# A third PSUM bank for the dilated heads' results, and the pair's transposes through one bank, a chunk every second step

## The chip, the cores and the metric

The kernel runs on one core of one Trainium2 chip. The metric is the device time in microseconds (us) of one execution; lower is better.

## The reference

One layer of a decoder trunk on `x` (1, 2048, 1024), fp32. `h = layer_norm(x)`, one projection `h @ w_in` is cut into the queries, keys and values of two mixers and a gate:

```python
proj = einsum('btd,dc->btc', h, w_in)
qa, ka, va, qb, kb, vb, gate = split(proj)
ya = dilated_mixture(heads_a(qa), heads_a(ka), heads_a(va), rel_bias)   # 8 heads of 64
yb = stick_breaking(heads_b(qb), heads_b(kb), heads_b(vb))              # 8 heads of 64
y = concatenate([ya, yb]) * silu(gate)
out = einsum('btc,cd->btd', y, w_out) + b_out
return layer_norm(ALPHA * h + out)
```

`dilated_mixture` runs every head in three configurations (window, dilation) = (128, 1), (512, 4), (2048, 16). In each, the 2048 positions are folded by residue into 16 tiles of 128 queries, and a tile attends to its own block of keys and the one before it (the first tile of a residue to its own alone), with a bias and a band mask, softmax with its own maximum and sum. The three outputs of a position are then merged, weighted by their softmax denominators.

## The kernel before

Four stages follow each other, each with its own tiles and one written order per engine: `front_phase` (layer norm, projection), `stick_phase` (the stick-breaking heads, and beside them the rest of the projection), `dilated_phase` (the eight dilated heads, the stage that the change edits) and `output_phase` (the output projection and the last layer norm).

**The dilated stage.** The heads go in four pairs, and a pair is one turn of 40 steps, 20 for each head (`par` 0 and 1). A step is one bunch: for dilation 16 (steps 0 to 3 of a head) four tiles of 128 keys, for dilation 4 (steps 4 to 11) and dilation 1 (steps 12 to 19) two tiles, of up to 256 keys each. In step s every engine runs, in this order:

- TensorE (PE): `scores` of bunch s (two products a tile, high and low part of the query), `transpose_weights` of bunch s-2, `values` of bunch s-4 (for every 128 keys one product with the high part of the transposed weights and one with the low part).
- ScalarE (ACT): `copy_low` (step s-5, where a bank of results is full), `high_part` of s-2, `weights` of s (the exponentials).
- VectorE (DVE): `minima` of s (bias and row minimum), `add_halves` (s-5, where a bank is full), `low_part` of s-2.

Results go to the PSUM banks `oa_ps`, four tiles to a bank, 12 banks' worth a head: with dilation 16 a bank is full after every step, later after every second. Before, there are two such banks: `values` that opens bank n waits until `add_halves` of bank n-2 (semaphore `rows_done`) has read it. `add_halves` puts the sums in `rows`.

**The merge.** Rows of dilation 16 and 4 lie in folded order. SyncE (SP) moves them back by DMA: `move_second` (through DRAM) and `move_first`, 16 small DMAs. DVE then runs `weigh_maxima` and `weigh_sums` (in steps 24 and 25 for the first head, in steps 4 and 5 of the next turn for the second), and GpSimd (POOL) the `merge` into `y_pos`. When both heads of a pair are merged, PE transposes `y_pos` in four chunks of four tiles into two banks `y_ps` (`transpose_pair`), DVE multiplies each chunk by the gate (`apply_gate`), and SP stores it (`finish`). Before, all four chunks go in step 13 of the next turn, PE and DVE alike. After the last pair the same is done at the end, chunk by chunk, by `merge_last` and `apply_gate` on DVE; the next stage reads what is stored there.

**Queries and keys of the next head.** `load_head` on SP loads them, `order` on POOL copies them into residue order for dilation 16 (two copies, `q_hi_res`, `q_lo_res`) and then for dilation 4 (three, with `k_res`). PE's `scores` wait for the first in step 0 of the head and for the second in step 4 (semaphore `ordered`).

SP runs, for each head, this list; it is the one on which much of the prediction rests (lines 1305 to 1325):

```python
load_head(*after)                       # queries, keys, bias of the next head
load_values(at(it, 2, par), 0)
rows_of(it, par, 2)                     # wait: rows of dilation 16 are there
load_values(after_head, 2)
move_second(it, par)
if par == 0 and not start:
    finish(at(it, 1, -1))               # four stores of the pair before, wait for them
    load_gate(it)
rows_of(it, par, 1)                     # wait: rows of dilation 4, added in step 16
move_first(it, par)
load_values(after_head, 1)
```

The turns of pairs 1 and 2 are a loop on every engine; pairs 0 and 3 are written out.

## Time and profile before

| | |
|---|---|
| median of 3 runs | 1766.65 us (1762.42 to 1768.78) |
| the profiled execution | 1758.86 us, its span 1757.0 us |
| mean granted clock of TensorE | 0.974 |
| PE busy | 1650.7 us (94% of the span) |
| DVE busy | 1172.8 us (67%) |
| ACT busy | 797.9 us (45%) |
| POOL busy | 330.9 us (19%) |
| the dilated stage | from about 1210 to 1563 us of the span |

A granted clock of 1.00 is 2.4 GHz, of 0.50 it is 1.2 GHz. "Idle before" is the time that an engine stood still just ahead of an instruction, with what ended it.

### The profile page before, as it was taken

The page shows a single profiled execution, that of the slowest core. Times are in us where ns is not written, and L with a number is a line of the kernel's source. Part 1 is how long each engine was busy: PE and PEld are TensorE (multiplying, and loading weights), DVE is VectorE, ACT ScalarE, POOL GpSimd, SP SyncE. Part 2 cuts the span into 40 slices and gives each one's busy share as a digit, 9 for nine tenths or more (in the row PEclk, how much of TensorE's full clock was granted, in tenths as well). Part 3 has the DMA queues.
Part 4 walks back from the last instruction along what each step waited for, and adds up shares of the span by engine and source line. Part 5 has one row for each costly group of instructions (what it writes and reads, how often), then busy time and mean ns, then how long its engine had stood idle before and what let it go on. Part 6 is the DMA issues. An engine that isn't in the chain of part 4 may idle for free. (4 is left out here: it accounts for less than half of the span.)

```text
span 1757.0 us, 27634 instructions
## 1 busy us (share of the span) xinstructions
PE 1650.7 (94%) x9138; PEld 1399.1 (80%) x9138; DVE 1172.8 (67%) x2323; ACT 797.9 (45%) x1993; POOL 330.9 (19%) x207
## 2 busy tenths in 40 slices
PE   5789999999979999999999999998999999949997
PEld 4577888888768888888878788887998998937886
DVE  5531124322326888888888888886887888865996
ACT  3341113211214555555555555555997888931000
POOL 2102100000000000000000000000576677501331
PEclk9899999999999999999999999998998999969999
DMA  4316966699739555755664575434677777456541
GB/s 170 142 58 214 332 240 222 209 274 293 254 147 264 164 179 182 249 157 170 196 213 156 157 201 165 154 108 132 197 212 206 229 230 204 127 168 212 180 144 60
DMA packets 222069, 332.48 MB, mean 189 GB/s; under 512 B 52269, under 2 KB 145896, under 8 KB 215596
## 3 DMA queue, kind: packets, MB, share of 16 engines
q1 hardware_dynamic: 217452, 321.35, 57.8%
q0 software_dynamic: 2400, 9.48, 1.7%
q8 instruction: 63, 1.03, 0.3%
q14 instruction: 74, 0.61, 0.1%
q10 hardware_dynamic: 2080, 0.01, 0.1%
HBM read 204.05 MB, written 122.39 MB: 186 GB/s over the span
## 5 line engine op out<-in xcount | busy, mean ns | idle before, releaser
L1049 ACT ACTIVATE WT_hi<-wt_ps 128x512 fp32r<-128x512 f32 (+1 forms) x320 | 171.1, 535 | 315.8 <-PE wt_ps L981 315.8
L1095 DVE TENSOR_TENSOR_SCAN W<-w,W,zeros 128x512 f32<-128x512 f32 x192 | 248.2, 1293 | 59.1 <-ACT w L1041 58.4
L379 PE MATMUL proj<-h_hi,w_hi 128*128 128x512 f32 x640 | 259.5, 405 | 19.8 <-DVE h_lo L555 16.0
L379 PE MATMUL proj<-h_hi,w_lo 128*128 128x512 f32 x640 | 252.4, 394 | 0.0
L379 PE MATMUL proj<-h_lo,w_hi 128*128 128x512 f32 x640 | 252.0, 394 | 0.0
L1103 DVE TENSOR_TENSOR WT_lo<-wt_ps,WT_hi 128x512 fp32r<-128x512 f32 (+1 forms) x320 | 187.3, 586 | 2.2 <-ACT WT_hi L1049 2.2
L1439 ACT ACTIVATE prob<-neg_s,rows 128x256 f32<-128x256 f32 (+1 forms) x384 | 173.5, 455 | 14.8 <-DVE rows L1499 13.2
L981 PE MATMUL wt_ps<-ident,W 128*128 128x128 f32 x1088 | 173.5, 275 | 6.7 <-DVE WT_lo L1103 5.9
L1041 ACT ACTIVATE w<-z_ps 128x512 f32<-128x512 f32 (+2 forms) x320 | 169.1, 528 | 20.5 <-PE z_ps L971 20.0
L981 PEld LDWEIGHTS wt_ps<-ident,W 128*128 128x128 f32 x1088 | 131.7, 140 | 43.3 <-DVE WT_lo L1103 15.5
L1401 PE MATMUL oa_ps<-va,PT_hi 128*128 128x128 f32 x600 | 150.4, 288 | 12.9 <-DVE rows L1517 12.7
L1017 PE MATMUL proj_a<-h_hi,wa_hi 128*128 128x512 f32 x384 | 152.7, 398 | 9.3 <-DMA wa_lo<-wa_d 9.2
L955 POOL TENSOR_TENSOR y_sum<-y_sum,gate 64x512 f32<-64x512 f32 x32 | 41.2, 1289 | 635.4 <-DVE y_sum L1110 635.4
L379 PEld LDWEIGHTS proj<-h_hi,w_hi 128*128 128x128 f32 x640 | 121.9, 190 | 47.5 <-DVE h_lo L555 17.9
L1017 PE MATMUL proj_a<-h_lo,wa_hi 128*128 128x512 f32 x384 | 153.2, 399 | 0.0
L1017 PE MATMUL proj_a<-h_hi,wa_lo 128*128 128x512 f32 x384 | 152.2, 396 | 0.0
L1499 DVE CUSTOM_DVE_ANT_0 neg_s<-s_ps,h_lo 128x256 f32<-128x256 f32 (+1 forms) x384 | 122.3, 362 | 41.3 <-PE s_ps L1376 37.9
L1095 DVE TENSOR_TENSOR_SCAN W<-w,ones_above 128x128 f32<-128x128 f32 (+3 forms) x128 | 114.2, 893 | 48.3 <-ACT w L1041 47.0
L1402 PE MATMUL oa_ps<-va,PT_lo 128*128 128x128 f32 x600 | 144.8, 278 | 0.0
L379 PEld LDWEIGHTS proj<-h_hi,w_lo 128*128 128x128 f32 x640 | 121.8, 190 | 26.7
L1000 PE MATMUL o_ps<-WT_hi,dv 128*128 128x512 f32 (+1 forms) x320 | 142.2, 444 | 0.0
L379 PEld LDWEIGHTS proj<-h_lo,w_hi 128*128 128x128 f32 x640 | 122.3, 191 | 23.3
(157 smaller groups left out, 3462.9 us busy)
## 6 DMA issues: line engine op xcount, KB each, us to landing
va_d<-st SPq DMA_DIRECT2D x96, 256.0 KB, 3.7
wa_hi<-wa_d SPq DMA_DIRECT2D x48, 512.0 KB, 3.8
wa_lo<-wa_d SPq DMA_DIRECT2D x48, 512.0 KB, 5.0
va<-va_d SPq DMA_DIRECT2D x24, 1024.0 KB, 8.1
wa_d<-x_sb SPq DMA_DIRECT2D x24, 512.0 KB, 3.8
w_raw<-in_w_tiles SPq DMA_DIRECT2D x18, 512.0 KB, 5.1
x_sb<-in_x SPq DMA_DIRECT2D x16, 512.0 KB, 5.8
qk_hi_d<-st SPq DMA_DIRECT2D x32, 256.0 KB, 2.8
```

What stands on the lines that cost most here:

```text
L379: last = pe.matmul(acc[n % ACC_SLOTS][:], w[w_slot(t)][:, k, :], h[ch][:, k, :], start=(k, a) == (0, 0), stop=(k, a) == (KD - 1, 2))
L981: last = pe.transpose(t_ps[n % T_SLOTS][:, i * P:(i + 1) * P], W[(QB * u + i) % W_SLOTS][:, j * P:(j + 1) * P], ident[:])
L1000: pe.matmul(o[:, cols], dv[h % 2][:, c * QB + j, :], WT_hi[n % PART_SLOTS][:, cols], start=False, stop=False)
L1017: last = pe.matmul(acc[a % 2][:], wt[a % 2][:, k, :], ht[ch % 2][:, k, :], start=rest == 0, stop=rest == KD * 3 - 1)
L1041: act.activation(w[n % W_IN][:, 0:width], z_ps[n % Z_SLOTS][:, 0:width], ACT.Sigmoid, scale=-SCALE).then_inc(w_done, 1)
L1049: act.activation(WT_hi[n % PART_SLOTS][:, cols], t_ps[n % T_SLOTS][:, cols], ACT.Copy) \
L1095: dve.tensor_tensor_scan(W[n % W_SLOTS][:, 0:width][:, ::-1], w[n % W_IN][:, 0:width][:, ::-1], above[:, ::-1], first, ALU.mult, ALU.max). ...
L1103: dve.tensor_tensor(WT_lo[n % PART_SLOTS][:, cols], t_ps[n % T_SLOTS][:, cols], WT_hi[n % PART_SLOTS][:, cols].bitcast(F32), ALU.subtract) ...
L1401: pe.matmul(out, PT_hi[b % PART_SLOTS][:, w], vk, start=(kb == 0), stop=False)
L1402: last = pe.matmul(out, PT_lo[b % PART_SLOTS][:, w], vk, start=False, stop=(kb == nk - 1))
L1439: last = act.activation(prob[b % SCORE_SLOTS][:, col:col + nk * P], neg_s[b % NEG_SLOTS][:, col:col + nk * P], ACT.Exp, scale=-1.0, bias=r ...
L1499: last = dve.tensor_tensor_reduce(out=neg_s[b % NEG_SLOTS][:, col:col + nk * P], in0=s_ps[b % 2][:, col:col + nk * P], in1=bias[par][:, c, ...
```

## The change

The third result bank is one of the two that the pair's transposes used: `oa_ps` has three, `y_ps` one. `values` that opens bank n now waits for `add_halves` of bank n-3. The pair's chunks are transposed in steps 13, 15, 17 and 19 and gated in steps 14, 16, 18 and 20; each transpose waits for the gate of the chunk before it, since there is one bank. On SP `finish` and `load_gate` go behind `move_first` and `load_values(after_head, 1)`, to the end of the first head's list. After the last pair the four chunks use the one bank too.

```diff
-    WEIGH_AT, PAIR_AT = 4, 13
+    WEIGH_AT = 4
+    PAIR_AT = (13, 15, 17, 19)
+    GATE_AT = tuple(s + 1 for s in PAIR_AT)
+    O_SLOTS = 3
...
-        o_ps, y_ps = m.banks("oa_ps", 2), m.banks("y_ps", 2)
+        o_ps, y_ps = m.banks("oa_ps", O_SLOTS), m.banks("y_ps", 1)
...
                 move_second(it, par)
-                if par == 0 and not start:
-                    finish(at(it, 1, -1))
-                    load_gate(it)
                 rows_of(it, par, 1)
                 move_first(it, par)
                 if not last:
                     load_values(after_head, 1)
+                if par == 0 and not start:
+                    finish(at(it, 1, -1))
+                    load_gate(it)
...
-                    out = o_ps[bank % 2][:, (idx % 4) * P:(idx % 4 + 1) * P]
+                    out = o_ps[bank % O_SLOTS][:, (idx % 4) * P:(idx % 4 + 1) * P]
...
-            def transpose_pair(pair, last_pair=False):
-                pe.wait_ge(merged, 1 + at(pair, 2, 1 if last_pair else 2))
-                for ch in range(NCH):
-                    if last_pair:
-                        pe.wait_ge(last_merged, ch + 1)
-                    pe.wait_ge(gated, at(pair, NCH, ch + 1))
-                    for j in range(4):
-                        last = pe.transpose(y_ps[ch % 2][:, j * P:(j + 1) * P],
-                                            y_pos[:, ch * 4 + j, :], ident[:])
-                    last.then_inc(y_done, 1)
+            def transpose_pair(pair, ch, last_pair=False):
+                if ch == 0:
+                    pe.wait_ge(merged, 1 + at(pair, 2, 1 if last_pair else 2))
+                if last_pair:
+                    pe.wait_ge(last_merged, ch + 1)
+                pe.wait_ge(gated, at(pair, NCH, ch + 2))
+                for j in range(4):
+                    last = pe.transpose(y_ps[0][:, j * P:(j + 1) * P],
+                                        y_pos[:, ch * 4 + j, :], ident[:])
+                last.then_inc(y_done, 1)
...
-                if s == PAIR_AT and before is not None:
-                    transpose_pair(before)
+                if before is not None and s in PAIR_AT:
+                    transpose_pair(before, PAIR_AT.index(s))
...
-            dve.sem_inc(rows_done, 2)
+            dve.sem_inc(rows_done, O_SLOTS)
...
-                if s == PAIR_AT and before is not None:
-                    for ch in range(NCH):
-                        apply_gate(before, ch)
+                if before is not None and s in GATE_AT:
+                    apply_gate(before, GATE_AT.index(s))
```

SP in the loop's turn, first head, from the write of the dilation 16 rows on. Before (L1290 and L1295 are `move_second`, L1268 `finish`, L1273 `load_gate`, L1302 `move_first`, L1263 `load_values`, L690 `load_head`):

```order
L1290 DMA move_d<-rows 128x1056
...
L1295 DMA moved<-move_d 128x16x66
...
L1268 DMA y_d<-gate_a 128x512
...
L1273 DMA gate_a<-gate_d 128x2048
L1286 REGISTER_ALU
L1302 DMA moved<-rows 32x4x66 x16
L1263 DMA va<-va_d 128x2048
L1281 ISA
L690 ISA
L690 DMA h_hi<-qk_hi_d 64x2048
```

With the change (lines four further on):

```order
L1294 DMA move_d<-rows 128x1056
...
L1299 DMA moved<-move_d 128x16x66
L1290 REGISTER_ALU
L1306 DMA moved<-rows 32x4x66 x16
L1267 DMA va<-va_d 128x2048
...
L1272 DMA y_d<-gate_a 128x512
...
L1277 DMA gate_a<-gate_d 128x2048
L1285 ISA
L690 ISA
L690 DMA h_hi<-qk_hi_d 64x2048
```

The stores of the pair before (one of the four shown) and the gate's load stood ahead of `move_first`; now they stand between the values' load and the next head's loads.

DVE in the loop's turn, where the gate was applied. Before, at the end of step 13:

```order
L1509 TENSOR_TENSOR PT_lo<-pt_ps,PT_hi 128x512
L1552 ISA
L1553 ISA
L1555 TENSOR_TENSOR gate_a<-y_ps,gate_a 128x512
L1553 REGISTER_ALU
L1555 TENSOR_TENSOR gate_a<-y_ps,gate_a 128x512
L1553 REGISTER_ALU
L1555 TENSOR_TENSOR gate_a<-y_ps,gate_a 128x512
L1553 REGISTER_ALU
L1555 TENSOR_TENSOR gate_a<-y_ps,gate_a 128x512
```

With the change, from the end of step 14 on:

```order
L1560 TENSOR_TENSOR gate_a<-y_ps,gate_a 128x512
...
L1514 TENSOR_TENSOR PT_lo<-pt_ps,PT_hi 128x512
...
L1522 TENSOR_TENSOR rows<-oa_ps,oa_low 128x4x64
L1514 TENSOR_TENSOR PT_lo<-pt_ps,PT_hi 128x512
L1558 REGISTER_ALU
L1560 TENSOR_TENSOR gate_a<-y_ps,gate_a 128x512
```

Four gates stood in one block at the end of step 13; now one stands at the end of every second step from 14 to 20.

## Rows read from the trace of the kernel before

**Rows 1.** Timeline of PE, pair transposes: start us, us, engine, line, what [idle before <-releaser]

```profile
1317.21 1.06 PE L1412 MATMUL y_ps<-ident,y_pos 128*128 128x128 f32 x8
...
1406.30 1.06 PE L1412 MATMUL y_ps<-ident,y_pos 128*128 128x128 f32 x8
1407.70 1.25 PE L1412 MATMUL y_ps<-ident,y_pos 128*128 128x128 f32 x8 [0.35 <-DVE gate_a L1555]
...
1486.87 1.06 PE L1412 MATMUL y_ps<-ident,y_pos 128*128 128x128 f32 x8
```

**Rows 2.** Waits of the stage, 1215 to 1563 us: total us, times, longest

```profile
PE oa_ps L1401 <- DVE rows L1517: 12.7, 14, 2.9
```

**Rows 3.** Timeline of PE around steps 27 to 29 of the last pair

```profile
1516.66 0.33 PE L1401 MATMUL oa_ps<-va,PT_hi 128*128 128x128 f32 x1 [1.12 <-DVE rows L1517]
...
1518.12 0.49 PE L1384 MATMUL pt_ps<-ident,prob 128*128 128x128 f32 x3
...
1519.60 0.60 PE L1384 MATMUL pt_ps<-ident,prob 128*128 128x128 f32 x4
```

**Rows 4.** Timeline of ACT, ends of the exponentials that these transposes need

```profile
1517.11 0.19 ACT L1439 ACTIVATION_READ_ACCUMULATOR prob<-neg_s,rows 128x1 f32 x1
...
1518.83 0.19 ACT L1439 ACTIVATION_READ_ACCUMULATOR prob<-neg_s,rows 128x1 f32 x1
```

**Rows 5.** Timelines of DVE and PE, weighing of the first head of pair 1

```profile
1344.41 0.19 DVE L1532 TENSOR_TENSOR neg_m<-rows,moved 128x16 f32<-128x16 f32 x1 [2.42 <-DMA moved<-rows]
...
1346.31 0.33 PE L1401 MATMUL oa_ps<-va,PT_hi 128*128 128x128 f32 x1 [2.92 <-DVE rows L1517]
```

**Rows 6.** A stretch: us, busy of PE, PEld, DVE, ACT, POOL, then PEclk, DMA, GB/s

```profile
1348.00:1361.65 13.65, 12.72 (x61) 12.33 (x60) 7.91 (x31) 7.67 (x27) 10.41 (x5) 0.50 1.02 219
```

**Rows 7.** Timeline of SP's queue, pair 1

```profile
1331.71 11.30 SPq L1302 DMA_DIRECT2D moved<-rows  x16
...
1343.96 0.55 SPq L690 DMA_DIRECT2D h_hi<-qk_hi_d  x1
```

**Rows 8.** Timeline of SP's queue, pair 2

```profile
1408.16 2.95 SPq L1268 DMA_DIRECT2D y_d<-gate_a  x4
1414.75 0.35 SPq L1273 DMA_DIRECT2D gate_a<-gate_d  x1
1415.21 10.55 SPq L1302 DMA_DIRECT2D moved<-rows  x16
...
1426.72 0.56 SPq L690 DMA_DIRECT2D h_hi<-qk_hi_d  x1
```

**Rows 9.** Timeline of DVE and PE, pairs 2 and 3: step 16; steps 0 and 4

```profile
1413.63 0.42 DVE L1517 TENSOR_TENSOR rows<-oa_ps,oa_low 128x256 f32<-128x256 f32 x1
...
1457.11 0.31 PE L1375 MATMUL s_ps<-h_hi,q_hi_res 128*128 128x128 f32 x1
...
1467.06 0.27 PE L1375 MATMUL s_ps<-k_res,q_hi_res 128*128 128x128 f32 x1
```

**Rows 10.** Timeline of POOL, first and last copy into residue order, pairs 1 and 2

```profile
1362.00 3.86 POOL L681 CAST q_hi_res<-h_hi 128x2048 fp32r<-128x2048 f32 x1 [2.82 <-DMA h_lo<-qk_lo_d]
...
1445.77 3.84 POOL L681 CAST q_hi_res<-h_hi 128x2048 fp32r<-128x2048 f32 x1
...
1461.20 3.98 POOL L681 CAST k_res<-h_hi 128x2048 fp32r<-128x2048 f32 x1
```

**Rows 11.** PE's wait at 106.88 us and the stretch around it

```profile
106.88 0.80 PE L379 MATMUL proj<-h_hi,w_hi 128*128 128x512 f32 x1 [3.26 <-DVE h_lo L555]
105.70:109.10 3.40, 2.22 (x5) 1.82 (x6) 1.38 (x2) 1.64 (x3) 0.00 (x0) 0.50 0.43 159
```

**Rows 12.** PE's wait at 1617.26 us and the stretch around it

```profile
1617.26 0.50 PE L1765 MATMUL out_ps<-wo_hi,y_hi 128*128 128x512 f32 x1 [1.75 <-DVE y_lo L1811]
1614.00:1618.00 4.00, 2.25 (x10) 1.59 (x9) 3.96 (x4) 2.12 (x2) 2.42 (x2) 1.00 0.19 77
```

**Rows 13.** Timeline of DVE and PE after the last pair

```profile
1551.20 0.68 DVE L1555 TENSOR_TENSOR gate_a<-y_ps,gate_a 128x512 f32<-128x512 f32 x1
1551.33 0.71 PEld L1412 LDWEIGHTS y_ps<-ident,y_pos 128*128 128x128 f32 x4 [1.31 <-DVE y_pos L1570]
```

More of the change, by code:

```diff
@@ L1285, in rows_of @@
             def rows_of(it, par, c):
-                sp.wait_ge(rows_done, 2 + at(it, 2 * OBANKS, par * OBANKS + bank_of(c, NTILE - 1) + 1))
+                sp.wait_ge(rows_done, O_SLOTS + at(it, 2 * OBANKS, par * OBANKS + bank_of(c, NTILE - 1) + 1))
             def move_second(it, par):
@@ L1422, in one_step @@
                     values(*then)
-                if s == PAIR_AT and before is not None:
-                    transpose_pair(before)
+                if before is not None and s in PAIR_AT:
+                    transpose_pair(before, PAIR_AT.index(s))
             run_turns(pe, one_step)
-            transpose_pair(PAIRS - 1, last_pair=True)
+            for ch in range(NCH):
+                transpose_pair(PAIRS - 1, ch, last_pair=True)
         @block.scalar
@@ L1453, in copy_low @@
                 act.wait_ge(pv_done, PART_SLOTS + at(it, STEPS, b + 1))
-                act.wait_ge(rows_done, at(it, 2 * OBANKS, n + 1))
-                src = o_ps[n % 2][:].rearrange("p (i a d) -> p i a d", i=4, a=2)
+                act.wait_ge(rows_done, at(it, 2 * OBANKS, n + 1 + O_SLOTS - 2))
+                src = o_ps[n % O_SLOTS][:].rearrange("p (i a d) -> p i a d", i=4, a=2)
                 act.activation(o_low[n % 2][:], src[:, :, 1, :], ACT.Copy).then_inc(low_copied, 1)
@@ L1514, in add_halves @@
                 dve.wait_ge(low_copied, 2 + at(it, 2 * OBANKS, n + 1))
-                src = o_ps[n % 2][:].rearrange("p (i a d) -> p i a d", i=4, a=2)
+                src = o_ps[n % O_SLOTS][:].rearrange("p (i a d) -> p i a d", i=4, a=2)
                 c, quad = ORDER[bank // 4], bank % 4
@@ L1554, in apply_gate @@
                 cols = gate[:, ch * CH:(ch + 1) * CH]
-                dve.tensor_tensor(cols, y_ps[ch % 2][:], cols, ALU.mult).then_inc(gated, 1)
+                dve.tensor_tensor(cols, y_ps[0][:], cols, ALU.mult).then_inc(gated, 1)
             def merge_last(ch):
```

## The prediction

> **What bounds the kernel now.** I read the stage that the change edits, first by its waits, then step by step on a timeline, then by granted clock. The page gives PE 94% of the span, so only PE's waits and its clock can return time here. In a step PE issues work without a pause; where it stands still, the row names who let it go.
>
> Three things hold PE up in this stage. First, the list of waits shows `values` waiting for `add_halves` 14 times, 12.7 us in all [rows 2]. These are two waits a head in seven heads, in steps 26 and 27 or 6 and 7, where DVE has the weighing besides its usual work. Second, one of them is long: in pair 1 DVE waited 2.42 us for the moved rows, and PE 2.92 us behind it [rows 5]. From 1348 us on TensorE then ran at the lower clock, 1.2 GHz, for 13.65 us although it was busy [rows 6]. Third, in step 13 the pair's 16 transposes wait for DVE's gates.
>
> The whole price of the second is in the length of a turn. From step 13 to step 13 it is 1406.30 - 1317.21 = 89.1 us for pair 1 and 1486.87 - 1406.30 = 80.6 us for pair 2 [rows 1]: 8.5 us more. Of these 2.4 are the wait, and about 6.1 the low clock.
>
> **The change part by part** (us, against the profiled execution's own 1758.86).
>
> *The third bank.* It takes the wait of `values` away, since bank n-3 was read a full step earlier. What is late next? In the last pair, `values` of step 27 began at 1516.66 after a wait of 1.12 [rows 3]. The transposes of step 28 began at 1518.12; they need exponentials that ACT ended at 1517.11 + 0.19 = 1517.30 [rows 3, 4]. So they can come 0.8 earlier, not 2. A step later it is 1519.60 against 1518.83 + 0.19 = 1519.02, 0.6 [rows 3, 4]. DVE and ACT are what PE meets next, and neither has less to do. I take 0.5 a head, seven heads: -3.5. The bounds are 0 and the 9.8 us that the 14 waits sum to without the 2.9; I stay near the low one because the rows of ACT are the nearest thing to what PE would wait for.
>
> *The transposes in four steps.* The 16 took from 1317.21, or 1406.30, to 1407.70 + 1.25 = 1408.95 [rows 1], 2.65 in all; the first eight took 1.06, so without a stop 16 need 2.1 at most, and less where the two halves overlap. 0.7 a pair, three pairs: -2.1 (bounds: -1.05, three idles of 0.35, and -2.6). The gates cost DVE the same 0.68 each [rows 13]; the list of waits has PE waiting for nothing in steps 14 to 20, so PE's own work hides them there. If that cover were gone, 2.7 us a pair would show.
>
> *After the last pair.* The second chunk's transposes began at 1551.33; with one bank they wait for the gate that ends at 1551.20 + 0.68 = 1551.88 [rows 13]. The same holds for the other two, and only the last shows at the end: +0.6.
>
> *The list on SP.* `move_first` no longer stands behind the stores, their wait and the gate's load. In pair 1 it began at 1331.71 and ran 11.30 us [rows 7], so its last part was issued at about 1342.4 and DVE went on at 1344.41 [rows 5]. Its rows come from step 16; in pair 2 that step's sum ended at 1413.63 + 0.42 = 1414.05 [rows 9], and pair 1 is 89.1 earlier, 1324.96. It can begin 6.7 earlier, which is more than the wait of 2.42. That wait goes, and the low clock behind it: -8.5 together. What is late next is DVE's own work.
>
> But `load_head` of the next pair now stands behind the stores. For pair 2, counted from 1414.05: `move_first` 10.6, the values' load 0.7, stores to gate 1414.75 - 1408.16 = 6.6, the gate 0.5, so `load_head` begins at 1432.5 and not at 1426.72 [rows 8]: 5.8 later. In pair 1 the same chain gives 1343.4, where it was 1343.96 [rows 7], but pair 2 now begins 8.5 earlier, so PE meets the same lateness. POOL can copy when the last load has landed: 1362.00 - 1343.96 = 18.0 after `load_head` began [rows 7, 10]. In pair 2 it was not seen waiting, and started 1445.77 - 1426.72 = 19.05 after [rows 8, 10], so 18 to 19 bounds it there from above. Now POOL starts at 1432.5 + 18.0 = 1450.5. Its five copies took 1461.20 + 3.98 - 1445.77 = 19.4 [rows 10], so the order for dilation 4 is there at 1469.9. Step 4 of pair 3 needed it at 1467.06 [rows 9]. The two chunks that move behind step 16 put this 0.9 later, the earlier `values` 0.5 earlier: PE waits about 2.4, partly already in step 0. Bounds: 1 if the loads land in 17, and 4.5 if the stores, now behind a 1 MB load, take 1 us more and the loads land in 19. I take 2.4 in pairs 2 and 3, of which 2.0 each stays (the DVE-bound steps behind catch some up): +4.0.
>
> *The clock once more.* A wait like this is near those after which the clock fell. At 106.88 us PE had waited 3.26, and the stretch shows 0.50 [rows 11]; 2.92 did it in pair 1 [rows 5, 6]. A wait of 1.75 left it at 1.00 [rows 12]. The new ones lie between, and there are two close together (step 0, step 4). I take a fall in both pairs as the likelier, at 6.1 less the 1.1 of waiting that a slower PE doesn't meet: 2 x 5.0 = +10.0.
>
> Sum: -3.5 - 2.1 + 0.6 - 8.5 + 4.0 + 10.0 = +0.5, so 1759.4 for an execution like the profiled one.
>
> **Profile and timed runs.** The profiled execution is 7.8 below the median and 3.6 below the fastest timed run. That distance is near the 6.1 of one fall, and the places where the trace is nearest to one are the pairs of waits for a bank, 3 us apart. I take it that the timed runs have one fall more there, which a third bank removes: 1766.65 + 0.5 - 6.1 = 1761.0. The trace itself shows no such fall between 1362 and 1542 us, so this is a reading of the times, not of a row. The Trainium skill, page "TensorE: Matmul & The Clock Gate", section "A second HAM failure mode: psum-queue depth-cycling", says that a kernel that cycles through PSUM banks can idle PE for short times so often that its clock goes up and down; by it the time would be 1761.0, by the profiled trace alone 1767.2. The same page, section "HAM oscillation — how this bites in real kernels", reports that PSUM double-buffering gave one kernel no further gain; by that the third bank would give 0 and not 3.5.
>
> **The rivals.**
>
> *A. Forecast, the returned gain, with the timed runs' further fall removed:* 1761.0.
>
> *B. The same, but what the timed runs have more is elsewhere:* 1766.65 + 0.5 = 1767.2. For it: the two-bank waits of the profiled execution made no fall of their own.
>
> *C. The new waits stay short or make one fall at most.* For it: nothing in the trace says what a wait between 1.75 and 2.92 does, and landing a little sooner takes a whole us off. Without falls and with waits of 1 each: -13.5 + 2.0 = -11.5, 1755.2; with one fall 1760.2.
>
> *D. Slower.* The queries' order on POOL becomes the bound: the stores, behind the values' load, and the loads, behind the gate's, take 2 us more than in [rows 8, 10]. PE then waits 4.5 in each of pairs 2 and 3, and both fall at the full 6.1, with one further fall in the loop: -13.5 + 9.0 + 12.2 = +7.7, 1774.4 (1780 with the further one). It decides from the point where both waits are over 2.9 and the timed runs lose nothing in return. Against it: POOL had 1.9 us to spare in pair 3 (1467.06 against 1465.18) [rows 9, 10].
>
> *E. The bank and the spread work, but the late rows stay,* because the DMAs of `move_first` land late, not start late, or something else ahead of them is late. Then -8.5 and the new waits' falls go together: about -5 + 4 = -1, 1765.7. Against it: the wait ended 2 us after the last issue [rows 5, 7].
>
> **How the numbers follow.** A 0.32, B 0.20, C 0.23, D 0.16, E 0.09. The predicted time is A's, 1761.0. About 0.3%, 5.3 us, is what a measurement of this kernel can tell from no change: faster means under 1761.35. A gives faster 0.19 and same 0.13 (it lies on the line), B same 0.19 and slower 0.01, C faster 0.22 and same 0.01, D slower 0.15 and same 0.01, E same 0.07, faster 0.01 and slower 0.01: faster 0.42, same 0.41, slower 0.17. The range goes from C's 1755 less its bounds to between B and D: 1752 to 1772. A and C alone would have 1752 to 1763.
>
> **What would show it.** The waits of `values` for `add_halves` are gone or under 2 us in all, and PE waits instead for the exponentials, 0.5 or so at a time. DVE's 2.42 for moved rows is gone and the clock stays at 1.00 at 1345 to 1362. On SP `move_first` stands right behind step 16's sum, and `load_head` some 18 us behind it. PE's first `scores` of dilation 16 or 4 in pairs 2 and 3 wait for POOL's copies, 2 to 3 us, and a stretch of 13 to 14 us at 0.50 follows. The prediction is wrong if these waits aren't there, if they leave the clock alone, or if the waits for a bank come back in another step.

## The result, and the profile after

| | before | after |
|---|---|---|
| median of 20 runs each, same chip, us | 1764.08 (1755.77 to 1773.94) | 1771.99 (1762.04 to 1784.54) |
| ratio after / before, 95% interval | | 1.0051 (1.0033 to 1.0068) |
| span of the profiled execution, granted clock | 1757.0, 0.974 | 1774.4, 0.964 |

The change made the kernel 0.5% slower. The forecast was 1761.0, below the kernel before, and its range ended at 1772, where the median lies.

What the change was made of did work. The list of waits of the stage, read again after the change, no longer has `values` waiting for DVE's rows, which were 12.7 us in 14 waits [rows 2]. At the head of what PE waits for stands something else:

```profile
L1405 PE MATMUL oa_ps<-va,PT_hi 128*128 128x128 f32 x600 | 158.3, 298 | 11.0 <-DMA va<-va_d 11.0
```

That is the page's row of the same `values` matmuls. The timeline of PE in pairs 1 and 2 (start, us, engine, line, operation, idle before it and releaser) shows where these 11.0 us lie; they are two waits, each at the first `values` of dilation 1 of a second head, where there was none before:

```profile
1373.48 0.47 PE L1405 MATMUL oa_ps<-va,PT_hi 128*128 128x128 f32 x1 [6.86 <-DMA va<-va_d]
...
1462.73 0.47 PE L1405 MATMUL oa_ps<-va,PT_hi 128*128 128x128 f32 x1 [4.17 <-DMA va<-va_d]
```

SP's queue in pair 1 says why they are late:

```profile
1330.13 11.78 SPq L1306 DMA_DIRECT2D moved<-rows  x16
1342.03 0.52 SPq L1267 DMA_DIRECT2D va<-va_d  x1
1342.84 2.43 SPq L1272 DMA_DIRECT2D y_d<-gate_a  x4
1351.21 0.35 SPq L1277 DMA_DIRECT2D gate_a<-gate_d  x1
1351.88 0.57 SPq L690 DMA_DIRECT2D h_hi<-qk_hi_d  x1
...
1356.89 1.84 SPq L1267 DMA_DIRECT2D va<-va_d  x2
```

The rows' move follows the first load of `moved` at once, as forecast, and DVE's wait of 2.42 for it [rows 5] is gone. But from the first store to the gate's load SP now stands for 1351.21 - 1342.84 = 8.4 us, against 6.6 before [rows 8], and the stores are behind a 1 MB load of values. `load_head` starts at 1351.88 instead of 1343.96 [rows 7], and behind it stands the load of the second head's own values of dilation 1, issued at 1356.89. PE asked for them at 1373.48 - 6.86 = 1366.62 and got them 16.6 us after their issue.

POOL's copies are late too, as the sum had it, but nobody meets that, since PE is held up for longer ahead of them:

```profile
1370.16 3.59 POOL L681 CAST q_hi_res<-h_hi 128x2048 fp32r<-128x2048 f32 x1 [8.50 <-DMA h_lo<-qk_lo_d]
```

Behind both waits TensorE ran for part of the time at the lower of its clocks (stretch, us, busy of PE, PEld, DVE, ACT, POOL, granted clock, DMA share, GB/s), and from 1500 us on at the full one again:

```profile
1366.00:1373.00 7.00, 0.62 (x6) 0.38 (x4) 1.96 (x7) 2.32 (x9) 2.84 (x1) 0.78 1.00 335
1373.00:1395.00 22.00, 20.57 (x133) 20.26 (x134) 11.50 (x54) 13.12 (x49) 16.18 (x5) 0.73 0.56 159
...
1463.00:1485.00 22.00, 21.15 (x137) 20.84 (x138) 11.71 (x54) 14.09 (x55) 15.42 (x5) 0.73 0.57 155
...
1500.00:1560.00 60.00, 57.13 (x503) 56.24 (x501) 51.36 (x199) 52.09 (x185) 32.87 (x12) 1.00 0.46 137
```

Where the 17.4 us between the two spans lie is read from the first transposes of each pair, as in [rows 1]. They begin at 1322.85, 1414.74 and 1503.68, where they began at 1317.21, 1406.30 and 1486.87. So 5.6 us come before the first of them, 2.8 from step 13 of pair 1 to step 13 of pair 2 (91.89 for 89.09), 8.4 from there to pair 3 (88.94 for 80.57) and 0.6 behind. The first 5.6 I don't put down to the change, because the clock differs where nothing was changed. This is the start of the stage in both profiles, after first:

```profile
1208.00:1244.00 36.00, 33.25 (x155) 33.28 (x156) 16.43 (x77) 20.82 (x75) 10.65 (x5) 0.53 0.85 250
```

```profile
1204.00:1240.00 36.00, 31.41 (x186) 30.16 (x185) 19.69 (x88) 24.63 (x85) 12.71 (x5) 0.81 0.81 249
```

The changed kernel has 34.1 us at 1.2 GHz there, and before 13.7. Over all kernels of this study that stretch was anything from 10.2 to 34.1 us long, with nothing changed in it. So one profile is better for the loop's turns than for the total, and totals below are medians. The turns are of one execution of each kernel too.

### The profile page after: what moved, and what is told of

It is laid out like the page before. It is cut to its first block and busy times, and to the rows that moved or that the text cites. A ratio compares the mean times of both kernels' runs of the same rounds, so it can differ in the third digit from the quotient of the medians.

```text
span 1774.4 us, 27634 instructions
## 1 busy us (share of the span) xinstructions
PE 1663.0 (94%) x9138; PEld 1414.2 (80%) x9138; DVE 1171.7 (66%) x2323; ACT 795.4 (45%) x1993; POOL 330.3 (19%) x207
## 5 line engine op out<-in xcount | busy, mean ns | idle before, releaser
L379 PE MATMUL proj<-h_hi,w_hi 128*128 128x512 f32 x640 | 258.9, 405 | 21.7 <-DVE h_lo L555 16.6
L1405 PE MATMUL oa_ps<-va,PT_hi 128*128 128x128 f32 x600 | 158.3, 298 | 11.0 <-DMA va<-va_d 11.0
L379 PEld LDWEIGHTS proj<-h_hi,w_hi 128*128 128x128 f32 x640 | 121.7, 190 | 49.3 <-DVE h_lo L555 18.2
L1406 PE MATMUL oa_ps<-va,PT_lo 128*128 128x128 f32 x600 | 153.0, 289 | 0.0
```

Source lines behind the costliest of these rows:

```text
L379: last = pe.matmul(acc[n % ACC_SLOTS][:], w[w_slot(t)][:, k, :], h[ch][:, k, :], start=(k, a) == (0, 0), stop=(k, a) == (KD - 1, 2))
L1405: pe.matmul(out, PT_hi[b % PART_SLOTS][:, w], vk, start=(kb == 0), stop=False)
L1406: last = pe.matmul(out, PT_lo[b % PART_SLOTS][:, w], vk, start=False, stop=(kb == nk - 1))
```

## The experiments

Theory Q: the order on SP is what costs, through the load of dilation 1's values; banks and spread give what the sum said. Rivals were that POOL's copies are the bound, and that the banks or the spread themselves do harm. Each result stands beside runs of the kernel before on the same chip: 1763.1, 1761.7, 1762.7 and 1761.1 us in the four groups of runs, in the order told here (e1 to e4, e5 to e8, e9 and e10, e11 and e12). The groups ran on four chips, so two kernels of different groups are compared by their distance from the kernel before of each. "Turns" are the two distances between the first transposes of the pairs in the profiled execution, 89.1 and 80.6 before, 91.9 and 88.9 after.

**e1. Stores and gate behind the second head's loads.** The changed kernel with

```
 (head, behind load_values(at(it, 2, par), 0))
+if par == 1 and not (isinstance(it, int) and it == 0):
+    finish(at(it, 1, -1))
+    load_gate(it)
 (head, at its end)
-if par == 0 and not start: finish(...); load_gate(it)
```

> The changed kernel with one thing moved: the stores of the pair before and the gate's load go on SP behind the second head's load_head and its load of the dilation 1 values. Theory Q (the queue): the loss of the change is the second head's values' load, which stands behind the stores, the gate's load and the next head's loads, so PE waits 6.9 and 4.2 us for it in pairs 1 and 2 and the clock falls behind both. Then these waits are gone here, DVE still doesn't wait for moved rows, and the time is 8 to 14 us below the kernel before, 1750 to 1756. Theory B (banks and spread): the third bank and the chunks in four steps lose the time themselves, and the waits for the load only take the place of other waits. Then the time stays within 3 us of the changed kernel, about 1770.

Measured: 1761.39 (1754.88 to 1764.86), ratio 0.9992 (0.9975 to 1.0009). All of the change's loss is gone, with banks and spread still in: theory Q holds in that. PE waits neither for values nor for a bank. But it is not the gain that the theory asked for, 8 to 14. PE's waits at the start of pairs 2 and 3, on its timeline, are new, and low clock follows both (10.2 and 13.7 us of it); turns 83.8 and 84.4.

```profile
1370.31 0.36 PE L1379 MATMUL s_ps<-h_hi,q_hi_res 128*128 128x128 f32 x1 [2.35 <-DVE rows L1504]
```

DVE was late in its turn, and its own row names nothing as the cause:

```profile
1369.33 0.29 DVE L1504 CUSTOM_DVE_ANT_0 neg_s<-s_ps,h_lo 128x128 f32<-128x128 f32 x1 [5.27 <-issue]
```

In the kernel before the same first minima of pair 2 wait too, but less:

```profile
1380.19 0.29 DVE L1499 CUSTOM_DVE_ANT_0 neg_s<-s_ps,h_lo 128x128 f32<-128x128 f32 x1 [3.24 <-PE s_ps L1376]
```

**e2. The order on SP alone.** The kernel before, two and two banks, with `finish` and `load_gate` where the change has them:

```
 move_second(it, par)
-if par == 0 and not start: finish(...); load_gate(it)
 rows_of(it, par, 1)
 move_first(it, par)
 if not last: load_values(after_head, 1)
+if par == 0 and not start: finish(...); load_gate(it)
```

> The kernel before with only the SP order of the change (stores and gate's load at the end of the first head's list); two result banks, two transpose banks, all chunks in step 13. Theory Q: the same waits of 4 to 7 us for the values' load in pairs 1 and 2, clock falls behind them, 5 to 12 us slower than before, since the waits for a bank are still there too. Theory B: the same as the kernel before or a few us faster, since the late rows of pair 1 are cured.

Measured: 1775.99 (1771.55 to 1779.99), ratio 1.0078 (1.0051 to 1.0104). The order alone costs 12.9 us. Its turns, 89.0 and 88.4, show 7.7 of that; where the timed runs lose the rest isn't seen. Its two waits are the change's, 5.99 and 5.44:

```profile
1372.37 0.47 PE L1401 MATMUL oa_ps<-va,PT_hi 128*128 128x128 f32 x1 [5.99 <-DMA va<-va_d]
```

Against the kernel before, e2 is 12.9 slower and the change 7.9. By that, banks and spread together bring 5.0, which is what the sum had, but the two intervals (1.0051 to 1.0104 and 1.0033 to 1.0068) overlap, so the times don't show it.

**e3. The values ahead of the queries.** The changed kernel, where the second head's `load_values(..., 0)` goes ahead of `load_head`:

```
-if not (start or last): load_head(*after)
+if not (start or last) and par == 0: load_head(*after)
 if not start: ... load_values(at(it, 2, par), 0)
+if not (start or last) and par == 1: load_head(*after)
```

> The changed kernel with one thing moved: in the second head's list the dilation 1 values are loaded ahead of load_head of the next pair. Theory Q: PE's waits for the values' load shrink from 6.9 and 4.2 us to under 1, as 2.6 MB no longer stand ahead of it; the queries of the next pair come 1 to 2 us later, and PE may wait up to 3 us for POOL's copies in step 0 or 4 of pairs 2 and 3. In all 4 to 10 us below the changed kernel, about 1765. Theory B: no more than 2 us below the changed kernel.

Measured: 1779.49 (1773.70 to 1783.52), ratio 1.0088 (1.0061 to 1.0114), slower than the changed kernel and not faster. The waits for values are gone, and POOL's copies are the bound at once; turns 94.9 and 91.9.

```profile
1382.24 0.47 PE L1381 MATMUL s_ps<-h_hi,q_hi_res 128*128 128x128 f32 x1 [8.48 <-POOL q_lo_res L681]
```

So neither of the two transfers can be late: the copies were next behind the values, and my sum had seen the second and not the first.

**e4. Two banks, stores behind the loads.** The kernel before with e1's place for `finish` and `load_gate`.

> The kernel before with only the stores and the gate's load moved to where e1 has them; two banks each, all chunks in step 13. Theory Q: the late rows of pair 1 (DVE 2.4 us, PE 2.9 us, then 13.65 us at half clock) are cured and nothing else changes: 5 to 8 us below before; the waits for a bank stay at some 1.4 us a head. The difference between e1 and this run is what the third bank and the spread are worth: 4 to 6 us. Theory B: e1 is no faster than this run.

Measured: 1763.93 (1756.11 to 1772.18), ratio 1.0000 (0.9978 to 1.0021). The 5 to 8 us that were expected did not come. Its late rows are gone as well, but DVE waits 5.49 at the start of pair 2, PE 2.57 behind it, and 13.7 us of low clock follow. Against e1 it is 2.5 slower, which is what banks and spread would be worth there; with spreads of 10 and 16 us over 12 runs each, that isn't clear of noise either.

**e5. Stores where the change has them, without waiting for them.** The changed kernel; the gate's load, with the wait for the stores, goes to the end of the second head's list (for the last pair it stays behind `load_values(..., 0)`):

```
 def finish(pair): ...
-    sp.wait_ge(y_stored, at(pair, 16 * NCH, 16 * NCH))
 def load_gate(pair):
+    sp.wait_ge(y_stored, ...)
 (head, at its end)
 if par == 0 and not start:
     finish(at(it, 1, -1))
-    load_gate(it)
+if par == 1 and not last and not (isinstance(it, int) and it == 0):
+    load_gate(it)
```

> The changed kernel with its pair's work on SP taken apart: the four stores are issued where the change issues them (behind the first head's list), but nothing waits for them there; the wait for the stores and the gate's load stand at the end of the second head's list (for the last pair behind that head's first load of values). THEORY (the blocking wait for the stores, 8.4 us, is what made the values of dilation 1 late, and the gate's load near the loop's boundary is what made DVE's first minima of a turn wait 5.3 us instead of 3.2): the head's loads start some 2 us behind where they start in the kernel before, the values land in time, PE's waits of 6.86 and 4.17 for va are under 1, DVE's first minima of a turn wait at most 3.5 and PE's scores at the turn's start under 1, and the time is 7 to 12 below the kernel before, 1751 to 1757. RIVAL 1 (the stores themselves, 1 MB in the queue ahead of the loads, are enough): the values are still 2 to 3 us late, a fall of the clock follows, 1762 to 1768. RIVAL 2 (falls come whatever is done): no wait over 1 us, but the low clock stays at 90 us or more and the time at 1758 to 1763.

Measured: 1762.30 (1755.73 to 1768.93), ratio 0.9995 (0.9973 to 1.0017). The time is rival 1's. `load_head` starts 2.9 us behind the first store instead of 9.0 (1348.54 - 1345.68), yet in pair 1 PE still waits for the values:

```profile
1372.19 0.47 PE L1410 MATMUL oa_ps<-va,PT_hi 128*128 128x128 f32 x1 [3.91 <-DMA va<-va_d]
```

So in pair 1 the 1 MB of stores itself, ahead of the loads in the rings, is enough. In pair 2 it is not: the values landed at 1456.2, and PE, 43.8 us behind its first transposes at 1413.13, wanted them at 1456.9.

**e6. Stores late and gate late.** e5 with the stores at e1's place.

> As the run with the stores behind the second head's loads (1761.4, waits of 2.35 and 2.04 at the start of a turn), with the gate's load alone moved on, to the end of the second head's list. THEORY (the gate's load and what it holds up, landing within 5 us of the turn's boundary, keep the DMA rings from fetching the engines' next instructions): DVE's first minima of a turn wait 3.0 to 3.5 instead of 5.3, PE's scores there under 1, and the time falls to 1752 to 1757. RIVAL (the wait at the boundary comes from the engines' lateness or from other loads): it stays at 2 or more and the time at 1759 to 1763.

Measured: 1755.87 (1751.01 to 1763.28), ratio 0.9969 (0.9950 to 0.9987): faster than the kernel before, turns 80.6 and 81.5. DVE waits 2.98 and 3.03 at the starts of pairs 2 and 3, and in the loop the clock stays at 1.00 throughout (stretch, columns as above):

```profile
1240.00:1540.00 300.00, 286.31 (x2466) 278.86 (x2465) 255.23 (x1050) 264.94 (x966) 202.09 (x69) 1.00 0.72 197
```

It shows one thing more: PE waited 2.29 and 3.31 for the values of dilation 1 of a first head, and the clock did not fall behind either. The second, on its timeline:

```profile
1493.26 0.32 PE L1410 MATMUL oa_ps<-va,PT_hi 128*128 128x128 f32 x1 [3.31 <-DMA va<-va_d]
```

**e7. The stores in their old place.** The changed kernel with `finish` and `load_gate` between `move_second` and `rows_of(it, par, 1)`, as before.

> The changed kernel with the stores and the gate's load put back on SP to where the kernel before has them, ahead of the first head's rows of dilation 4: third bank and transposes in four steps alone. THEORY (the last chunk is ready only at step 20, so stores, their landing and the gate's load hold up the rows' moves by 10 us or more, and with them the weights, the loads of the head and the values): DVE waits 8 to 14 us for the moved rows in every pair but the first and last, POOL's copies are late too, and the time is 1780 to 1800. RIVAL (the moves have slack): 1760 to 1770.

Measured: 1780.17 (1777.37 to 1780.81), ratio 1.0099 (1.0072 to 1.0126). Banks and spread without the new order are worse than all three together: chunk 3 is now gated in step 20, and with it the rows come late in each of the three pairs. DVE's timeline, and PE's behind it:

```profile
1345.15 0.19 DVE L1537 TENSOR_TENSOR neg_m<-rows,moved 128x16 f32<-128x16 f32 x1 [6.57 <-DMA moved<-rows]
```

```profile
1346.72 0.58 PE L1379 MATMUL s_ps<-k_res,q_hi_res 128*128 128x256 f32 x1 [5.92 <-DVE rows L1504]
```

The spread, then, can't be had without moving the stores.

**e8. The bank alone.** The kernel before with three banks for the results and one for the transposes, all four chunks in step 13:

```
-o_ps, y_ps = m.banks("oa_ps", 2), m.banks("y_ps", 2)
+o_ps, y_ps = m.banks("oa_ps", 3), m.banks("y_ps", 1)
-pe.wait_ge(gated, at(pair, NCH, ch + 1))
+pe.wait_ge(gated, at(pair, NCH, ch + 2))
 (and the counts of rows_done that go with them)
```

> The kernel before with the third bank for the results and one bank for the pair's transposes, all four chunks still in step 13, and its own order on SP. THEORY: PE's waits for DVE's rows (12.7 in pairs 1 to 3) go and 0.3 to 0.5 a head for the exponentials comes, worth 3 to 4 us over the program; the transposes of chunks 1 to 3 now each wait for the gate of the chunk before (about 1 us each, 3 us a pair, three pairs), which gives it back; the moved rows stay late in pair 1. 1762 to 1767. RIVAL 1: the bank's gain stands and the transposes' waits are covered: 1757 to 1760. RIVAL 2: the waits between chunks bring a fall of the clock in every pair: 1770 to 1780.

Measured: 1771.49 (1764.46 to 1775.17), ratio 1.0057 (1.0036 to 1.0079). It is slower than the theory's 1762 to 1767, at a time that was rival 2's. The list of waits shows the bank's waits gone and the transposes' in their place, three a pair and three more at the end:

```profile
PE y_ps L1412 <- DVE gate_a L1555: 12.2, 12, 1.6
```

In step 13 of each pair they are 0.91 + 0.79 + 0.78 = 2.5, 7.5 in all. The clock fell behind those of pair 1 alone, for 3.4 us, so rival 2's fall in every pair isn't in the profile. Pair 1's late rows, expected to stay, are gone: DVE began to weigh at 1347.99 without a wait, 28.7 us behind the pair's first transposes, where before it was 27.2 with 2.42 of waiting in it. DVE also waited 4.47 at the start of pair 2. The profiled execution is the fastest of its runs, so what the others lose beyond this is not seen; their granted clock is 0.9685 in the median against 0.973. A third bank taken from the transposes, without the spread, loses.

**e9. The gate behind the next values.** e6 with the gate's load, for pair 0 too, in the next pair's first list behind `load_values(..., 0)`.

> As the run with stores and gate late (1755.9), with the gate's load moved on once more: behind the loads of the next head and of its values of dilation 1 (for pair 0 too; the last pair's behind its second head's values). THEORY (that run's only long waits left, 2.29 and 3.31 for va in the second half of a turn, come from the gate's 1 MB queued in front of the loads of head and values): they go to under 0.7, nothing else moves, and the time is 4 to 6 lower, 1750 to 1753, with no low clock between the start of the stage and the last pair's end. RIVAL (the gate now lands too late, or holds up the rows of dilation 16 on their way out and back): DVE waits for the gate at step 14 or for the moved rows at step 17, PE's scores behind it 2 or more, and the time stays at 1755 to 1762.

Measured: 1760.06 (1753.10 to 1767.43), ratio 0.9982 (0.9959 to 1.0005). The time is the rival's and not the 1750 to 1753 of the theory. The waits for values are gone as the theory had it, and the second turn is the shortest of all, 79.2 (the first is 86.1). The rival's late gate is there once, in pair 1: DVE waited 1.74 for it, PE 1.55 behind it. But at the start of pair 2 DVE waited 4.77 (PE 1.85, then 13.7 us of low clock), which e6 had not. So where the gate's load stands was not what made e1's boundary slow.

**e10. Two banks in e9's order.**

> The kernel before, with its two and two banks and its transposes in step 13, with exactly the order on SP of the run with the gate behind the values. It says what third bank and spread transposes are worth under an order on SP in which no transfer is late. THEORY (my sum's terms: 3.5 for the banks, 2.1 for the transposes, 0.6 given back, and no clock fall behind waits of 1.1): 4 to 6 slower than its partner with three banks, 1755 to 1758, and itself 4 to 8 faster than the kernel before. RIVAL 1 (bank waits alone bring falls of the clock in each pair): 10 or more slower than its partner. RIVAL 2 (banks are worth nothing once the queue is in order): within 2 of it.

Measured: 1769.64 (1763.19 to 1771.97), ratio 1.0034 (1.0016 to 1.0052). It is 9.6 slower than e9, near rival 1's 10, but not for the banks alone. All four chunks are wanted in step 13, and the gate's load lands 2 to 4 us behind it, so PE waits 4.03 and 2.37 there in pairs 1 and 2. The comparison doesn't give the banks' worth.

**What the boundary depends on.** The eleven profiles were then read at one place: the microsecond behind a turn's last operation on DVE, and DVE's wait that begins there. e3 is left out, because its wait there is POOL's.

| kernel, start of pair 2 / of pair 3 | share of the DMA rings in that us | DVE waits, us |
|---|---|---|
| e6, both | 0.07 / 0.36 | 2.98 / 3.03 |
| before, both | 0.26 / 0.26 | 3.24 / 2.96 |
| after, both | 0.41 / 0.41 | 3.25 / 3.15 |
| pair 3 of e4, e10, e9 | 0.12, 0.29, 0.25 | 3.49, 3.38, 3.22 |
| pair 2 of e10, pair 3 of e5 | 0.46, 0.64 | 3.65, 3.90 |
| e1, both | 0.88 / 0.87 | 5.27 / 4.96 |
| pair 2 of e4, e9, e8 | 0.95, 1.26, 1.34 | 5.49, 4.77, 4.47 |

The places that aren't shown (both of e2 and e7, pair 3 of e8, pair 2 of e5) have shares of 0.25 to 0.37 and waits of 2.96 to 3.29. Transfers that are in the rings when the engines go back to the loop's start go with a longer wait. e11 and e12 test that from both sides.

**e11. A copy at the boundary.** The kernel before, plus 1 MB from memory to memory, which nothing needs:

```
 for g ... for r ...:  (move_first)
     sp.dma_start(moved[...], rows[...])
+    if par == 1 and (g, r) == (1, 1):
+        ... (wait for the copy of the turn before)
+        sp.dma_start(extra_d[:, :], gate_d[0:P, :])
```

> The kernel before with one copy of 1 MB from memory to memory (the gate's block into a tensor that nobody reads) issued by SP after the sixth of the 16 pieces of the second head's rows of dilation 4, some 2 us ahead of the end of a turn's instructions. In the eleven profiles so far the rings were 0.26 and 0.26 busy in the microsecond behind the turn's last operation on DVE in the kernel before, and DVE's first minima of the next turn then waited 3.24 and 2.96; in the five boundaries with a share of 0.87 or more it waited 4.47 to 5.49. THEORY (transfers that are in the rings when the engines turn back to the start of the loop hold up what the engines must fetch there): the share at the boundary is 0.8 or more, DVE waits 4.5 to 5.5, PE's scores behind it 1 to 2.5, and the time is 3 to 15 above the kernel before, with the clock's falls. RIVAL (the long waits at the boundary came with the late engines, not from the rings): the wait stays at 3.0 to 3.3 and the time within 3 of the kernel before.

Measured: 1764.79 (1758.96 to 1773.14), ratio 1.0023 (1.0007 to 1.0039), turns 93.1 and 91.7. DVE's first minima, PE's scores behind them, and the stretch at the boundary (the share that this view gives can be over 1):

```profile
1378.48 0.29 DVE L1506 CUSTOM_DVE_ANT_0 neg_s<-s_ps,h_lo 128x128 f32<-128x128 f32 x1 [5.93 <-issue]
```

```profile
1379.47 0.48 PE L1382 MATMUL s_ps<-h_hi,q_hi_res 128*128 128x128 f32 x1 [3.01 <-DVE rows L1506]
```

```profile
1372.50:1373.50 1.00, 1.00 (x12) 1.00 (x11) 0.05 (x1) 0.39 (x2) 1.00 (x1) 1.00 3.12 983
```

The theory holds: 5.93 and 5.60, more than the 4.5 to 5.5 expected, with 13.7 and 27.3 us of low clock behind. The copy was issued at 1371.45 and landed 6.3 us later, at 1377.7; DVE went on at 1378.48. In the timed runs it cost 3.7 us, the low end of what was expected.

The trace also shows what the copy held up. Its transfers have a kind, and a few of them, of 8 or 16 KB, are "instruction". From 1372.6 to 1376.0 there is none of these, only the copy's packets (packets, MB, share):

```profile
q1 hardware_dynamic: 16, 1.05, 97.0%
```

In the kernel before, the same place, 1377.0 to 1378.2, has two:

```profile
q14 instruction: 2, 0.02, 5.6%
```

**e12. The rows out first.** e9, with the second head's list reordered:

```
 (second head) load_head; load_values(..., 0)
-finish; rows_of(it, par, 2); load_values(after_head, 2); move_d<-rows; moved<-move_d
+rows_of(it, par, 2); move_d<-rows; finish; load_values(after_head, 2); moved<-move_d
```

> The run with the gate behind the values (1760.1), with the second head's list changed once more: its rows of dilation 16 go out ahead of the stores and of the next head's values of dilation 16, so that their way back ends before the turn does (there it began 2.2 us ahead of the turn's end in pair 1). THEORY (what is left in that run is the wait of 4.77 at the boundary of pair 1 and the fall behind it): the rings' share in the microsecond behind a turn's end is under 0.5, DVE waits there 3.0 to 3.3 in both pairs, PE's scores under 0.5, no va wait over 0.7, no low clock between the stage's start and the last pair's end, and the time is 1750 to 1755. RIVAL 1 (stores and values are now themselves in the rings at the turn's end): a wait of 4 to 5.5 stays, 1757 to 1762. RIVAL 2 (SP, which sits between the rows' way out and back, now issues the later list too late): va or moved rows late by 2 or more, 1760 to 1770.

Measured: 1754.21 (1748.91 to 1759.64), ratio 0.9964 (0.9946 to 0.9981), the lowest of all: 6.9 below the kernel before, where the changed kernel is 7.9 above, some 15 us apart. Turns 81.2 and 81.7; no wait of PE in the loop for rows of a bank or for values, two behind the gate (1.55 and 0.90), 3.4 us of low clock. The rings were 0.42 and 0.25 busy at the boundary, and DVE waited:

```profile
1374.67 0.29 DVE L1510 CUSTOM_DVE_ANT_0 neg_s<-s_ps,h_lo 128x128 f32<-128x128 f32 x1 [3.50 <-PE s_ps L1386]
```

```profile
1455.02 0.29 DVE L1510 CUSTOM_DVE_ANT_0 neg_s<-s_ps,h_lo 128x128 f32<-128x128 f32 x1 [3.22 <-PE s_ps L1386]
```

Its ratio and e6's (0.9969) are too near to be told apart, and its interval overlaps e9's (0.9959 to 1.0005) as well: that it beats the kernel before is shown, that the last step did it is not.

## Why the prediction was wrong

**What bounds it, and the third bank.** Right. The 12.7 us of `values` behind DVE's rows are gone, and PE meets the exponentials instead: 2.7 in 7 waits (1.2 in 2 before), and 1.8 in 6 for the slots of the scores (0.3 in 1 before). Its timeline after has 0.30 at a time, the sum had 0.5 a head:

```profile
1352.60 0.55 PE L1388 MATMUL pt_ps<-ident,prob 128*128 128x128 f32 x3 [0.30 <-ACT prob L1444]
...
1532.41 0.33 PE L1379 MATMUL s_ps<-k_res,q_hi_res 128*128 128x128 f32 x1 [0.35 <-DVE rows L1504]
```

**The transposes in four steps, and the end.** Right in place: PE waits for no gate in steps 13 to 19. At the end its three waits are 1.61 + 1.56 + 1.56 where they were 0.91 + 1.53 + 1.53, 0.8 more for the 0.6 forecast:

```profile
1567.75 1.08 PE L1416 MATMUL y_ps<-ident,y_pos 128*128 128x128 f32 x4 [1.61 <-DVE gate_a L1560]
```

The sum took 0.7 a pair for the spread, and its rows give 2.65 - 2.12 = 0.5. Together with the bank -5.0 was forecast; e2 against the change gives -5.0, e4 against e1 -2.5, and neither is clear of noise. The waits show the mechanism; its worth in time stays open.

**The late rows.** Right. DVE's 2.42 and the fall behind it are gone after, in e1 and in e4.

**`load_head` later, POOL's copies, 2.4 each.** This is the step that failed: the term of +4.0 for PE's wait for POOL's copies. It followed one of the transfers behind the stores, the one for POOL, and stopped there. The list has another right behind it: the second head's own values of dilation 1. This is their load on SP's queue in pair 2 of the kernel before:

```profile
1432.14 0.33 SPq L1263 DMA_DIRECT2D va<-va_d  x1
```

At the 16.6 us that the same load took in pair 1 of the changed kernel, they were there at 1448.7. PE asks for them 43.8 us after the pair's first transposes (1366.62 - 1322.85, and in pair 2 1458.56 - 1414.74), which was 1450.1: 1.4 us to spare. With the forecast's own delay of 5.8 that is a wait of 4.4. The changed kernel's was 4.17 in pair 2. So the reader was the wrong one. The delay was near in pair 2, in part by luck: the stores took 8.6 from the first to the gate (1441.09 - 1432.52) and not 6.6, which is what rival D had feared, but `move_first` had begun earlier than forecast, so that `load_head` was 6.6 later against the pair's first transposes (1441.76 - 1414.74 for 1426.72 - 1406.30) for the 5.8 forecast, and the values landed in 15.7 and not 16.6. In pair 1 the stores took 8.4, `load_head` was 29.0 behind the first transposes (1351.88 - 1322.85), and the wait was 6.86. PE's 11.0 for values stand in the place of the 4.0 for copies. e2 shows that the order, with these waits and what they set off, is the loss, and e1 that without it none of the loss is left. e3 shows that the copies were the next reader, no further than the values' waits away. The sum's 18.0 from `load_head` to POOL's first copy held, 18.3 and 17.6 in the changed kernel; had PE not been held up before, its step 4 of pair 3 would have waited about 3 us for the copies (an estimate: 1459.40 + 19.4 less 1414.74 + 60.8, less 0.4).

**The clock once more.** Right that it falls behind both waits. Between 1366 and 1500 us the changed kernel had about 37 us at 1.2 GHz, and before 13.7 us in all of its turns. The forecast had two falls like the one before.

**Rival D** had the right sign and nearly the size (+7.7, measured +7.9), by the wrong reader; its point of decision, waits over 2.9 in both pairs, was met.

**Profile and timed runs, -6.1.** This is the second term that failed. Nothing supports it. I had put the distance between the profiled execution and the median down to a fall at the waits for a bank. No profile with two banks shows such a fall: e2, e4, e10 and e11 have their low clock behind late values, gates or rows, or at a turn's start. In the 20 timed runs of the kernel before, two (1755.77 and 1758.25) are below the profiled execution's 1758.86, so it lies at the low end of the usual spread and no more. And all profiles show 10.2 to 34.1 us of low clock at the stage's start, and in the 20 runs of the changed kernel a mean clock lower by 0.001 goes with 1.2 us more. A part of the spread lies there, whatever the banks; the timed runs have no trace, so where the rest lies stays open. Without this term the forecast would have been 1767.2, rival B's.

**The page on bank cycling** (the Trainium skill, "TensorE: Matmul & The Clock Gate", section "A second HAM failure mode: psum-queue depth-cycling") describes short waits for banks that make the clock swing. In this kernel two such waits a head, up to 1.1 us each, did not; the measurement decides.

## What to carry to other kernels

When a block is moved on a DMA queue, list every transfer that it is moved ahead of, with who reads each and when, and cost the one with the least time to spare; here two readers were each within a few us of being late, and only one was counted. Then look at what is in the rings when a loop turns back: the order in which no reader was late (e1) gained nothing, and the two that left that moment clear at both turns (e6, e12) are the ones that gained. And a small gain on the engine that bounds (here 2.5 to 5 us, not clear of noise) is easily less than what the reordering that it needs can cost (12.9).

## What the runs showed of the hardware

**The loop's end.** DVE waits 2.96 to 3.50 us there with quiet rings (share up to 0.42 in the microsecond behind its last operation), 3.65 and 3.90 at 0.46 and 0.64, and 4.47 to 5.93 with full ones. PE then waits 1.55 to 3.01 for it. e11 shows that a transfer at that moment lengthens the wait. The traces point to what is held up. At each of the 26 boundaries of the table, e11 and e12, take the first three transfers of kind "instruction" that start no more than 0.6 us ahead of the turn's last operation on DVE. The last of them is over 0.8 to 1.8 us behind that operation in the 19 places with waits up to 3.90, and 2.3 to 4.1 behind it in the seven from 4.47 up, and DVE goes on 1.6 to 2.2 us after it in all 26. That the engines wait for these transfers fits every boundary; which engine's instructions each of them carries isn't in the trace.

**The clock behind waits.** At the start of a pair, waits of PE of 0.57 and 2.57 (e4), 0.98 (e5), 1.55 (e8), 1.85 (e9), 2.04 and 2.35 (e1), 2.68 and 3.01 (e11) were each followed by 10.2 to 27.3 us at 1.2 GHz, though PE was busy in them. At the same place 0.58 (e12) and 0.73 (e10) were followed by none, and in the middle of a pair 2.29 and 3.31 (e6) weren't either. The length of a wait alone does not tell.

**Stores behind loads.** What waits for four stores of 256 KB to land was issued 6.6 us after the first store in the kernel before, 8.4 and 8.6 after it behind one load of 1 MB in the changed kernel, and 18.2 after it in e1 (1338.76 to 1357.00), behind a head's loads and its values.
